# Order of TensorE's work in an attention step: the values ahead of the next unit's turn

## The reference

```python
def mla_attention(...):     # 4 heads
    s = jnp.where(kpos[None, :] <= qpos[:, None], s, NEG)
    p = jax.nn.softmax(s, axis=-1).astype(v.dtype)
    return jnp.einsum('bhqk,bkhd->bqhd', p, v)
def diff_attention(...):    # 4 heads, two maps each
    p = jax.nn.softmax(s, axis=-1)
    a = p[:, :, 0] - lam * p[:, :, 1]
    return jnp.einsum('bhqk,bkhd->bqhd', a.astype(v.dtype), v)
def nsa_attention(...):     # 8 heads, three branches each
    ...
    o = gt[..., 0:1] * o_cmp + gt[..., 1:2] * o_slc + gt[..., 2:3] * o_win
```

## Time and profile before

| what | value |
|---|---|
| median of 3 runs | 3538.94 us (3538.66 to 3551.74) |
| profiled execution | 3536.8 us, its span 3534.8 us |
| TensorE busy | 3448.3 us, 98% of the span |
| VectorE, ScalarE, GpSimd busy | 1662.3, 1477.1, 1549.6 us |
| attention of the first layer | 537.3 to 705.0 us of the span |
| attention of the second layer | 1605.7 to 1772.7 us |

### The profile page before, as it was taken

The page is one execution under the profiler, slowest core; times in us unless marked ns, Lnnn a source line. Parts: engine busy times, 40 slices in busy tenths (PEclk is TensorE's granted clock), DMA queues, the critical chain, the costliest instruction groups (busy, mean ns, idle before and its releaser), DMA issues.

```text
span 3534.8 us, 56010 instructions
## 1 busy us (share of the span) xinstructions
PE 3448.3 (98%) x21291; PEld 2892.9 (82%) x21291; DVE 1662.3 (47%) x2762; ACT 1477.1 (42%) x2450; POOL 1549.6 (44%) x1384
## 2 busy tenths in 40 slices
PE   8999999999999999999999999999999999999998
PEld 7899776589998999776588997888888785778887
DVE  8456635475657565644575656111112504661112
ACT  5344435554545354535554544312112335443223
POOL 4555545445545554545445554323323542034443
PEclk9999999999999999999999999999999999999999
DMA  4343444223433343444223333222222323023332
GB/s 125 107 113 90 108 125 126 90 72 107 112 90 95 97 119 87 104 122 142 90 60 107 107 92 100 67 63 66 60 61 58 93 56 101 19 62 99 95 95 66
DMA packets 569569, 322.57 MB, mean 91 GB/s; under 512 B 30282, under 2 KB 563376, under 8 KB 569008
## 3 DMA queue, kind: packets, MB, share of 16 engines
q1 hardware_dynamic: 569392, 320.22, 31.7%
HBM read 318.08 MB, written 2.10 MB: 91 GB/s over the span
## 4 chain that ended last, share of the span: by engine, by line
PE 63%; issue 22%; POOL 8%; DVE 3%; ACT 1%; DMA 1%; POOLq 0%; ACTq 0%; DVEq 0%
PE psum L3108 20%; PE psum L3001 16%; PE psum L3215 12%; POOL w_lo L993 7%; PE psum L3421 2%; PE psum L3498 2%; PE psum L3455 1%; PE psum L3395 1%; PE psum L3142 1%; PE psum L3145 1%; PE psum L3523 1%; PE psum L3262 1%; PE psum L3540 1%; DMA ada_raw<-ada_w 1%; POOL set_lo L1048 0%
## 5 line engine op out<-in xcount | busy, mean ns | idle before, releaser
L993 POOL TENSOR_TENSOR w_lo<-w_raw,w_hi 128x512 fp32r<-128x512 f32 x488 | 656.2, 1367 | 1102.0 <-ACT w_hi L1085 1101.9
L1085 ACT ACTIVATE w_hi<-w_raw 128x1024 fp32r<-128x1024 f32 x244 | 257.5, 1058 | 836.6 <-PE psum L3001 714.8
L3001 PE MATMUL psum<-h_hi,w_hi 128*128 128x512 f32 x1136 | 452.2, 398 | 1.6 <-POOL w_lo L993 1.6
L3001 PE MATMUL psum<-h_hi,w_lo 128*128 128x512 f32 x1136 | 442.9, 390 | 0.0
L3001 PE MATMUL psum<-h_lo,w_hi 128*128 128x512 f32 x1136 | 442.5, 390 | 0.0
L1048 POOL TENSOR_TENSOR set_lo<-w_raw,set_hi 128x512 fp32r<-128x512 f32 x224 | 292.5, 1335 | 222.1 <-ACT set_hi L1164 219.1
L3108 PE MATMUL psum<-t_hi,set_hi 128*128 128x256 f32 x1280 | 361.2, 282 | 10.7 <-ACT gated L1154 8.7
L3108 PE MATMUL psum<-t_hi,set_lo 128*128 128x256 f32 x1280 | 360.1, 281 | 0.0
L3108 PE MATMUL psum<-t_lo,set_hi 128*128 128x256 f32 x1280 | 359.7, 281 | 0.0
L3215 PE MATMUL psum<-a_hi,set_hi 128*128 128x512 f32 x704 | 276.9, 393 | 2.9 <-DVE a_lo L2150 2.9
L3215 PE MATMUL psum<-a_hi,set_lo 128*128 128x512 f32 x704 | 274.2, 390 | 0.0
(11 more groups left out here) (628 smaller groups left out, 8115.9 us busy)
## 6 DMA issues: line engine op xcount, KB each, us to landing
w_raw<-ffn_w SPq DMA_DIRECT2D x120, 512.0 KB, 3.8
w_raw<-ffn_w_gate SPq DMA_DIRECT2D x88, 512.0 KB, 4.1
w_raw<-ffn_w_up SPq DMA_DIRECT2D x88, 512.0 KB, 4.0
ada_raw<-ada_w SPq DMA_DIRECT2D x72, 512.0 KB, 4.7
w_raw<-ffn_w_down SPq DMA_DIRECT2D x64, 512.0 KB, 3.9
w_raw<-w_in SPq DMA_DIRECT2D x60, 512.0 KB, 3.8
w_raw<-ffn_w_down SPq DMA_DIRECT2D x32, 384.0 KB, 3.2
w_raw<-w_out SPq DMA_DIRECT2D x24, 512.0 KB, 3.6
```

Source lines behind the costliest of these rows:

```text
L993: last = nc.gpsimd.tensor_tensor(w_lo[:, i, at], w_raw[:, i, at], w_hi[:, i, at].bitcast(F32), ALU.subtract)
L1085: nc.scalar.activation(w_hi[:, pos, :], w_raw[:, pos, :], ACT.Copy).then_inc(hi_ready, 1)
L3001: last = nc.tensor.matmul(dst, w[:, pos, k * P:(k + 1) * P], rhs[g][r](k0 + k), start=k == 0 and m == 0, stop=k == nk - 1 and m == 2)
```

## The change

In each step the values of unit t-4 are issued ahead of the turn of unit t-3 and, in step 6, of the compressed turn. The waits of steps 10 and 11 stay directly ahead of the values, and so come ahead of the turn. No instruction, wait or buffer is added or removed, and the other engines' programs are the same. The moved block, cut:

```diff
                         last.then_inc(ada_turned.sem, 1)
-                    u = t - X_LAG
-                    if 0 <= u < NU:
-                        pe.wait_ge(*unit_scaled(layer, u))
-                        ...
-                            for b in range(TILE_AT[u // UN] + 1):
-                                last = nc.tensor.transpose(psum[:, 4 + slot, b * P:(b + 1) * P], probs[:, u % 3, m, b * P:(b + 1) * P], ident[:])
-                            last.then_inc(probs_turned.sem, 1)
                     if t < NU:
-                        if step == AT_CMP_TURN:
-                            ...
-                            last.then_inc(cmp_turned.sem, 1)
                         if step == AT_FIRST:
...
                                 last = nc.tensor.matmul(o_place(kind, h), v(b), probs_t[e % 2][:, x, b * P:(b + 1) * P],
                                                         start=first and b == 0, stop=final and b == TILE_AT[j])
                         last.then_inc(o_done.sem, 1)
+                    u = t - X_LAG
+                    if 0 <= u < NU:
+                        pe.wait_ge(*unit_scaled(layer, u))
+                        ...
+                            last.then_inc(probs_turned.sem, 1)
+                    if t < NU:
+                        if step == AT_CMP_TURN:
+                            ...
+                            last.then_inc(cmp_turned.sem, 1)
                     if t < NU and step == AT_FIRST + 1:
                         for half in range(2):
```

More of the change, by code:

```diff
@@ L3442, in attention @@
                         last.then_inc(ada_turned.sem, 1)
-                    u = t - X_LAG
-                    if 0 <= u < NU:
-                        pe.wait_ge(*unit_scaled(layer, u))
[L3446 to L3453, removed]
-                            for b in range(TILE_AT[u // UN] + 1):
-                                last = nc.tensor.transpose(psum[:, 4 + slot, b * P:(b + 1) * P], probs[:, u % 3, m, b * P:(b + 1) * P], ident[:])
-                            last.then_inc(probs_turned.sem, 1)
-                    if t < NU:
-                        if step == AT_CMP_TURN:
[L3459 to L3463, removed]
-                            last.then_inc(cmp_turned.sem, 1)
+                    if t < NU:
                         if step == AT_FIRST:
@@ L3500, in attention @@
                         last.then_inc(o_done.sem, 1)
+                    u = t - X_LAG
+                    if 0 <= u < NU:
+                        pe.wait_ge(*unit_scaled(layer, u))
+                        e, slots = event_of(u), unit_slots(u)
+                        x = TURN_AT["unit", e]
+                        for m, slot in enumerate(slots):
+                            if x and slot == 0:
+                                pe.wait_ge(*first_turn_read(layer, x - 1))
+                            if e and slot == 1:
+                                pe.wait_ge(*probs_t_dve(layer, e))
+                            for b in range(TILE_AT[u // UN] + 1):
+                                last = nc.tensor.transpose(psum[:, 4 + slot, b * P:(b + 1) * P], probs[:, u % 3, m, b * P:(b + 1) * P], ident[:])
+                            last.then_inc(probs_turned.sem, 1)
+                    if t < NU:
+                        if step == AT_CMP_TURN:
+                            pe.wait_ge(*cmp_scaled(layer, i + 1))
+                            pe.wait_ge(*first_turn_read(layer, TURN_AT["cmp", i] - 1))
+                            for g in range(NSA_G):
+                                last = nc.tensor.transpose(psum[:, 4, g * P:(g + 1) * P],
+                                                           cmp_p[:, 4 * g:4 * g + 4, :].rearrange("p h n -> p (h n)"), ident[:])
+                            last.then_inc(cmp_turned.sem, 1)
                     if t < NU and step == AT_FIRST + 1:
```

## The result

The changed kernel takes 3592.99 us (median; 3579.24 to 3596.34), the kernel before 3540.37: a ratio of 1.0139, 95% interval 1.012 to 1.0158 (the two medians alone give 1.0149). The kernel before has a fourth run by now, hence 3540.37 for 3538.94. The change costs 52.6 us where 29.5 were forecast (21.5 for stalls and 8 for the clock); 3593 lies 9 us above the range.

A forecast was written before the change was run, and what follows sets the result against it. TensorE was taken to bound the kernel, its work unchanged. The profiled 3536.8 us plus 21.5 of stalls and 8 of clock gave 3566.3; with 2.1 for the median, 3568 us, range 3549 to 3584.

The forecast's parts named there:

- stalls: Attention stage, both layers: TensorE's added waits, 10.75 us a layer, 21.5 for two; bounds 10 and 31.
- the clock: Attention: about eleven new idles, one fall in two, 1.7 us each, 9 us, taken as 8.
- Step 11: Each tile: TensorE waits for h_lo ahead of the values, 5.16 us a layer; bounds 2.6 and 6.4.
- The end: Last four steps, without scores: 0.61 us exposed in each, 2.45 us a layer; bounds 1.7 and 3.2.
- Step 3 and the first tile: Ada's sums at L3440 wait for mod_rows, 3.72 us a layer; values in the first tile's step 4, +0.38.
- the chain through GpSimd to L3462: Step 3 at 128 keys: POOL's first scaling starts 2.6 us late, TensorE meets it at L3462, 2.14 us.
- Ordinary steps and cmp_pt: Ordinary steps cost nothing, copies stay covered; values fill step 7's wait for cmp_pt, -0.96 us a layer.
- The upper bound of 19: Upper bound in us of the cost of clock falls in the attention; lower bound 0.
- The third rival: Clock alternates: falls follow nearly each of the eleven idles, 3580 to 3592 us; chance 0.11.
- The first rival: ScalarE's and VectorE's free time takes stalls back: 10 us of stalls, no clock fall, 3549 us; chance 0.20.
- the second: Rival: values fill the turns' waits and nothing slips, gain some 1.2 us a layer, 3536 us; chance 0.03.
- The fourth: Rival: the order does nothing because TensorE's queue holds it elsewhere, 3539 us; chance 0.04.

The follow-up runs named there:

- experiment 1: Kernel before, with values ahead of the turn only in steps 10 and 11 of each tile: 3562.37 us, ratio 1.0063.
- experiment 5: Kernel before, with values ahead of the turn only in steps 1 to 4 of each tile: 3553.99 us, ratio 1.0044.
- experiment 2: Changed kernel, but with the turn ahead of the values as before in steps 10 and 11 of each tile: 3565.92 us, ratio 1.006.
- experiment 3: Kernel before, with values first only in the last steps of each layer's attention, which have no scores: 3545.68 us, ratio 1.0006.
- experiment 4: Kernel before, with values first only in steps 0, 5 to 9, 12 and 13 of each tile: 3545.97 us, ratio 1.0016.
- experiment 7: Changed kernel with 1, 4, 1 and 2 extra pairs of score products in step 11 (tiles of 512, 128, 384, 256 keys): 3580.86 us, ratio 1.0118.
- experiment 11: Changed kernel with ada's turned sums (L3434 to L3442) issued behind the turns: 3567.33 us, ratio 1.0087.
- experiment 12: Changed kernel with ada's turned sums behind the turns and the extra score products of experiment 7 in step 11: 3549.24 us, ratio 1.0041.
- experiment 10: Kernel before with ada's turned sums behind the turns, and values first in step 7 of each tile alone: 3525.37 us, ratio 0.9958.
- experiment 8: Kernel before with ada's turned sums (L3434 to L3442) moved behind the turns of their step: 3527.33 us, ratio 0.9971.

## Why the prediction was right in its direction and too small

**What bounds the kernel: right.** TensorE's idle time and clock decide; its work is the same, and VectorE's, ScalarE's and GpSimd's busy times moved by 2 us at most.

**Stalls: 21.5 forecast, 23.2 measured.** The sum is right, its terms less so:
- *Step 11* (10.3 us for both layers): 9.6 by experiment 1, and the idle time grew by 4.7 and 5.2 us a layer for 5.16. The forecast of 1.8 to 1.9 us a wait was a little high, it is 1.70 at full clock. (Its upper bound, all of the values block on top of the turns, is 6.2 us a layer by the rows and not 6.4.)
- *The end* (4.9): 5.3, with four waits of 0.61 us as worked out.
- *Step 3 and the first tile* (2 times 3.72 and 0.38, 8.2 us): 4.8 by experiment 5. The wait ahead of L3440 grew by 2.0 us a layer, not to "about 5". At 384 keys it grew from 1.28 to 1.52 us (0.24 for a forecast of 0.37), at 256 keys from 0.3 to 1.04 (0.7 for 1.21); at 128 keys the chain through GpSimd to L3462, worth 2.14 (a figure for which the text gives no full working), doesn't occur: no wait of that size is in the list, only 1.09 us ahead of L3440 itself. The values' wait in the first tile is 0.86 us, where the turn waited 0.31 before.
- *Ordinary steps and cmp_pt* (nothing, and -1.9 us): +4.2. The text named the test itself, a step longer than 3.40 us at 512 keys; it takes 3.54. But what failed is not the cover. No wait stands in the step: scores to values take 1.28 us where scores to turn took 1.19, the turn 1.02 for 0.97. Step 7 of the same tile has the same loss, 2.89 us for 2.74. I read it so that passing from one kind of work to the next takes TensorE some hundredths of a microsecond, which differ with the pair; no experiment took that apart. I had priced a moved block by its own duration, as if what stands beside it didn't matter.

The last two errors, 3.4 us too much and 6.1 too little, cancel in part.

**The clock: 8 forecast, 27 measured. This is the term that failed**, in the step "at one fall in two and 1.7 us each". The number and the length were both too low. The clock's record of the profiled execution has eleven low stretches in the two attentions, four of 6.8 to 17.1 us in the first layer and seven of 3.4 to 10.2 in the second, 99 us in all, where the kernel before had three and 20 us. That is eight falls more, where I had taken eleven new idles and half as many falls, and 9 us each where I took 3.4. (The trace has ten waits of 1 us and more that weren't there or were shorter than that, and four that grew.) I had halved the shortest of the three stretches that the earlier trace rows and the text knew (3.4, 6.8, 10.2), though their mean was 6.8. With eight falls at half of 9 us the term is 36 us, which is what the profiled execution shows (its clock cost 61 us, before 25); the four runs' mean is 27.

The upper bound of 19 was the same 1.7 us for every idle, so it was no bound: a bound has to take the longest stretch seen.

Where the falls stand, the trace tells too. All six waits ahead of L3440 (1.04 to 1.52 us) have one: a low stretch begins within 2.1 us of their end, 51 us of low clock in all. Of the six DMA waits of 1 us and more three have one, 34 us, and of the eight waits of step 11 only two, 14 us, though seven of these last 1.70 us. The other profiled executions agree. Counted over all fourteen, a low stretch begins during a wait or within 2.5 us behind it at 31 of the 38 waits of 1 us and more ahead of L3440, at 10 of the 24 waits of step 11 that are longer than 1.1 us, at none of the 19 there between 1.04 and 1.07 us, and at 23 of the 79 DMA waits of 1 us and more. The forecast priced all new idles alike; by this they are not alike. And the halves of experiments 1 and 2 are by edit and not by idle: turning steps 10 and 11 costs half of the clock's loss, but its falls stand in part behind waits elsewhere.

The third rival (3580 to 3592), to which I gave 0.11, is what happened, and a little beyond. The text had cited for it the Trainium skill, page "TensorE: Matmul & The Clock Gate", section "A second HAM failure mode: psum-queue depth-cycling", that frequent short idles between groups of matmuls make the clock alternate. The runs bear out the effect, and not that short idles as such cause it: the idles of 0.61 us cost no clock (experiment 3: -1.4 us), the short gaps of ordinary steps none that can be told from nothing (experiment 4: +2.3), and the loss goes with the edits that make or fill the idles of 1.0 to 1.7 us (experiments 1, 5, 7, 11, 12).

**The first rival** (stalls of 10 us, no fall) and the second (a gain) did not come: the waits that the values fill are 0.7 us a layer, and experiment 10 shows no gain at full clock from them. The fourth is refuted by the order in the rows.

**What stays open.** Why one idle makes the clock fall and another doesn't. In experiment 8 DMA waits of up to 2.03 us are left, and the clock is 1.00 all through; in experiment 1 the same waits had different outcomes in the two layers. Length alone doesn't decide; the place matters, as the counts above show, and no run here varied the work around an idle of constant length. Open too are the busy time of the ordinary steps, and what is left of experiment 11's gap, where 6.6 us of waits went, 4.9 us of idle time, and 2 us of stalls.

## What to carry to other kernels

Where TensorE is the bound, price a new idle of a microsecond or more twice: by its length, and by the low clock behind it, with the mean and the longest low stretch that the trace shows and not with the shortest. Look first which of the present waits have a low stretch behind them: here both long waits ahead of L3440 had one in the kernel before (1.28 and 1.27 us). Split each measured time into span times clock and the rest; it tells at once which of the two an edit moved. And look at TensorE's existing long waits for a block that can be issued ahead of them: moving one such wait behind a turn gave 0.29% in this kernel, some 10 us (4.5 of stalls and 5.8 of clock).

## What the runs showed of the hardware

- Work without use can be free or better: 16 pairs of extra score products in two layers' idles took 12 us off the changed kernel's median, all of it clock (experiment 7: cost 45.6 us against 56.5, four runs each); with ada's block moved as well they took 18 us off (experiment 12 against 11, clock's cost 21.0 against 37.5).
- Taking 1 us of waits ahead of L3440 out of each layer left no low stretch in the attention of one profiled execution (experiment 8), and TensorE's busy time for the same work went from 157.1 to 151.4 us. It isn't so in every execution: in that of experiment 10, which has the same move, the clock was 0.93 in the first layer and 1.00 in the second.
- The clock's loss is spread by chance: with the same waits one layer ran at 0.87 and the other at 0.97 (experiment 1), and the runs of the changed kernel differ by 17 us, at mean clocks of 0.982 to 0.988.
- In the changed kernel's profiled execution a fall came behind six of six waits of 1.04 to 1.52 us ahead of L3440, behind two of eight waits in step 11 (seven of them of 1.70 us), and behind three of the six DMA waits of 1 us and more; over all profiled executions it is 31 of 38 ahead of L3440, and 10 of 24 in step 11. The length of an idle alone doesn't tell whether the clock falls.
- The order of blocks costs TensorE time without any wait: 3.54 us against 3.40 for the same instructions of one step.
